# MoE expert weights of a two-layer encoder: gate and up matrix loaded as one array of 32 KB rows into four alternating places

## Chip, cores and metric

One core of one Trainium2 chip. The metric is the device time of one execution in microseconds (us). The profile is of one such execution.

## The reference, cut to what matters

All values are float32: x is 256 tokens by 1024. Each of the two layers is a token mixer (attention in layer 0, gated linear attention in layer 1) with a residual, then a hierarchical mixture of experts (MoE) with a residual:

```python
def hierarchical_moe(h, w_grp, b_grp, w_exp, b_exp, w_gate, w_up, w_down):
    ...   # top 1 of 4 groups, top 2 of its 8 experts: gates[token, expert]
    for e in range(N_EXPERTS):                       # 32 experts
        hid = jax.nn.silu(h @ w_gate[e]) * (h @ w_up[e])         # 1024 x 512 each
        y = y + gates[..., e:e + 1] * (hid @ w_down[e])          # 512 x 1024
```

Each of the three matrices of an expert is 2 MB (2^20 bytes to the MB where sizes of matrices are told), so a layer reads 32 x 6 = 192 MB of expert weights, which fit on the chip only a few at a time.

## The kernel before

**Rounds.** A layer's MoE runs in 11 rounds, r = 0 to 10. A light round handles three experts with 32 token slots each, round 8 (`HEAVY_ROUND`) the two experts with the most tokens, with 64 slots each. Experts 0 to 5 are taken in rounds 0 and 1 whatever the routing says; the list `order`, which DVE works out from the routing, names the later ones.

**TensorE in a round** (`expert_round`). `expand("gate")`: 24 products of 512 columns (48 matmul records), the weights as the moving operand. Then `scatter` of the round before into the sum (8 records, 96x512), `turn_gates` in even rounds, `expand("up")`, four transposes of `hid` (L2334), in odd rounds `gather` of the tokens of the next group (`ahead`), and the product with down (48 records). Round 0 is written apart (`expand_first`): gate and up in four quarters of the contraction.

**Places in SBUF.** `unit[0..8]` are nine places of 2 MB (16 KB on each of 128 partitions): gate in 0 to 2, up in 3 to 5, down in 6 to 8. The mixers use units 0 to 5 for their input projection and units 3 and 4 for the output projection. Two more places, `held` and `held_down`, lie in the arena that the mixers share; in each layer they take gate and down of expert 3 for round 1 and then stay empty until the next layer.

**What sets the order of the loads.** All of them are issued by SP in program order, on one queue. Each waits for a semaphore that TensorE raises when a kind of matrix has been used: `used["gate"]`, `used["up"]`, `used["down"]` (in round 0 also `quarter_used` and `up_quarter_used` after each quarter). SP blocks at the first wait that isn't met, and what stands behind it in the program isn't issued. In `later_round` SP waits for gate of the round before and issues three gates, waits for up and issues three ups, waits for down and issues three downs. On the other side TensorE waits for each kind's arrival alone (`arrived`). `second_round` refills the places of round 0 quarter by quarter for round 1, and then loads the first expert of round 2 in advance.

Of the kernel before, what the change touches and what calls it, by code (L numbers as in the profile page):

```python
# [19 lines left out]
P = 128  # L20
F32 = mybir.dt.float32
I32 = mybir.dt.int32
ALU = mybir.AluOpType
# [3 lines left out]
SEQ, D = 256, 1024  # L27
TILES = SEQ // P
KT = D // P
# [25 lines left out]
KINDS = ("gate", "up", "down")  # L55

# [5 lines left out]
GROUP = 2 * LIGHT  # L62
GROUP_SLOTS = 2 * ROUND_SLOTS
# [10 lines left out]
UNIT = 8 * HALF  # L74
IN_UNITS = 6
# [128 lines left out]
def by_block(w):  # L204

    layers = w.shape[0]
    return np.ascontiguousarray(w.reshape(layers, EXPERTS, KT, P, D_EXPERT).transpose(0, 1, 3, 2, 4)
                                ).reshape(layers, EXPERTS, P, UNIT)
# [10 lines left out]
def build(nc, A, out):  # L219
    ctx = ExitStack()  # L220
    with ctx:
# [145 lines left out]
        gfin = held[:, 0:D]  # L367
        y = hn
        moe_sum = hn
        up_rows_of = (up_rows, hn.rearrange("p t n -> p (t n)"))  # L370
# [4 lines left out]
        held_full = sem("held_full")  # L375
        held_down_full = sem("held_down_full")
        quarter_used, up_quarter_used, up_early_full = sem("quarter_used"), sem("up_quarter_used"), sem("up_early_full")
        up_rows_full = sem("up_rows_full")
        early_full = sem("early_full")
        first_full = [sem(f"first_full{b}") for b in range(2)]  # L380
        last_full = [sem(f"last_full{i}") for i in range(len(LAST_PARTS))]
        last_up = [sem(f"last_up{h}") for h in range(2)]
# [54 lines left out]
        class PassSems:  # L437


            def __init__(self, name, started, apart, held):  # L440
# [6 lines left out]
                self.held = held  # L447
                self.full = {kind: sem(f"{name}_{kind}_full") for kind in KINDS}
# [21 lines left out]
        main = PassSems("main", 0, {"gate": 2, "up": LIGHT, "down": 2 + LIGHT}, {"gate": 2, "up": 0, "down": 2})  # L470
        more = PassSems("more", 1, {"gate": 0, "up": 0, "down": 0}, {"gate": 0, "up": 0, "down": 0})
# [10 lines left out]
        OUT_UNITS = (3, 4)  # L482
# [64 lines left out]
        def _(sp):  # L547
# [3 lines left out]
            def mixer_weights(layer):  # L551

                for c in range(IN_UNITS):
                    if layer == 1:
                        sp.wait_ge(main.used[KINDS[c // 3]], ROUNDS)
# [17 lines left out]
                for c in range(LIGHT):  # L573
                    sp.wait_ge(proj_psum, 2 * IN_UNITS * layer + 2 * c + 2)
                    known(layer, "gate", c, unit[SLOT["gate"] + c], main.full["gate"])
                    if layer and c == 0:
                        half_rows(layer, "up", 0, 0, up_rows_of[0], up_rows_full)
# [1878 lines left out]
```

## Time and profile before

| | |
|---|---|
| three runs | 1180.72, 1181.81, 1183.72 us; median 1181.81 |
| the profiled execution | 1182.63 us, of it 1180.8 us between its first and last instruction |
| busy | TensorE matmul (PE) 84%, weight loads (PEld) 39%, DVE 24%, ACT 11%, POOL 1% |
| chain of work that ended last | PE 50%, DMA 43%, DVE 3%, SP 2% |
| HBM | 440.5 MB read, 374 GB/s over the span |

The span is cut in 40 slices of 29.5 us in the profile's second part: a digit is a busy share in tenths. Layer 0's MoE runs from about 156 to 583 us, layer 1's from 745 to 1172 us. In the timelines a row is a group of consecutive instructions of one engine: start, duration from the first start to the last end, engine and line, operation, operands and count, and in brackets the idle time before it and who ended it. "SPq ... DMA_DIRECT2D" is SP issuing a DMA. The view of busy time by stretch has, in each row: start and end, length, busy us and count of instructions of PE, PEld, DVE, ACT and POOL, the granted clock of TensorE as a share, the busy share of the 16 DMA engines, and GB/s.

### The profile page before, as it was taken

To read this page: it belongs to the slowest core of one execution; us is meant where nothing else is said; L and a number is where in the kernel's file an instruction comes from. 1 tells how busy PE (TensorE), PEld (TensorE's weight loads), DVE (VectorE), ACT (ScalarE), POOL (GpSimd) and SP (SyncE) were. 2 spreads that over 40 slices of the span, in tenths; PEclk is the share of its full clock that TensorE was granted. 3 is DMA by queue.
4 is the path that set the end of the run, shared out by engine and by line. 5 is a ranking of instruction groups with operands and counts; after the bars stand their busy time and mean duration, and the time that the engine had idled before them with its cause. 6 is when DMAs were issued, how large, how long until landed. Compare 5 with 4: busy or idle time off the path is not lost.

```text
span 1180.8 us, 12753 instructions
## 1 busy us (share of the span) xinstructions
PE 994.1 (84%) x5268; PEld 455.1 (39%) x5268; DVE 288.1 (24%) x677; ACT 125.9 (11%) x307; POOL 7.1 (1%) x12
## 2 busy tenths in 40 slices
PE   9999999966776777977999999999667767788876
PEld 8675653323223223342484546433132132232422
DVE  1265352201101101220322453522111111112212
ACT  2024010000000000000231121100000000000002
POOL 0000000000000000000000000000000000000000
PEclk9999999989879879988999999999898898899888
DMA  9923999999999999999983528899999999999995
GB/s 368 409 81 135 420 360 428 426 428 428 428 427 428 429 427 427 427 424 423 413 353 136 214 72 369 331 428 427 427 428 429 428 428 428 428 428 426 424 422 225
DMA packets 39297, 442.43 MB, mean 375 GB/s; under 512 B 4386, under 2 KB 4770, under 8 KB 11972
## 3 DMA queue, kind: packets, MB, share of 16 engines
q1 hardware_dynamic: 39092, 441.47, 89.7%
q8 instruction: 40, 0.66, 0.2%
q10 hardware_dynamic: 144, 0.12, 0.0%
q14 instruction: 21, 0.17, 0.0%
HBM read 440.53 MB, written 1.05 MB: 374 GB/s over the span
## 4 chain that ended last, share of the span: by engine, by line
PE 50%; DMA 43%; DVE 3%; SPq 2%; issue 2%; ACT 0%; DVEq 0%; POOL 0%
PE psum L1739 48%; DMA sb_weights<-moe_w_down 38%; DMA sb_weights<-moe_w_gate 5%; SPq L673 1%; SPq L679 1%; DMA sb_lead<-lead 0%; PE psum L2334 0%; DVE sb_weights L1598 0%; PE psum L1917 0%; PE psum L1750 0%; DVE sb_x L1618 0%; PE psum L1777 0%; PE psum L2112 0%; PE psum L2015 0%; PE psum L2202 0%
## 5 line engine op out<-in xcount | busy, mean ns | idle before, releaser
L1739 PE MATMUL psum<-sb_weights,sb_hT 128*32 128x512 f32 (+3 forms) x2352 | 468.7, 627 | 99.8 <-DMA sb_weights<-moe_w_gate 61.2
L1739 PE MATMUL psum<-sb_weights 128*32 128x512 f32 (+12 forms) x1632 | 318.7, 560 | 46.1 <-DMA sb_weights<-moe_w_down 41.0
L1739 PEld LDWEIGHTS psum<-sb_weights,sb_hT 128*32 128x32 f32 (+2 forms) x2352 | 148.1, 128 | 392.3 <-issue 313.5
L1739 PEld LDWEIGHTS psum<-sb_weights 128*32 128x32 f32 (+7 forms) x1632 | 115.8, 138 | 237.2 <-issue 195.3
L1611 DVE TENSOR_TENSOR sb_hn<-sb_hn,psum 128x512 f32<-128x512 f32 x72 | 49.5, 687 | 228.2 <-PE psum L1739 228.0
L1739 PE MATMUL psum<-sb_hT,sb_weights 128*128 128x256 f32 (+1 forms) x400 | 88.8, 380 | 0.1
L1739 PEld LDWEIGHTS psum<-sb_hT,sb_weights 128*128 128x128 f32 (+1 forms) x400 | 74.0, 187 | 12.6 <-issue 1.6
L1739 PE MATMUL psum<-sb_weights,sb_x 128*128 128x192 f32 (+2 forms) x448 | 69.6, 313 | 6.7 <-issue 6.1
L1739 PEld LDWEIGHTS psum<-sb_weights,sb_x 128*128 128x128 f32 x448 | 66.7, 197 | 11.5 <-issue 10.3
L1603 DVE COPY sb_weights<-psum 96x512 f32<-96x512 f32 (+1 forms) x20 | 13.7, 686 | 181.0 <-PE psum L1739 181.0
L1598 DVE TENSOR_TENSOR sb_weights<-sb_weights,psum 96x512 f32<-96x512 f32 (+1 forms) x22 | 15.0, 683 | 148.9 <-PE psum L1739 148.9
L920 ACT ACTIVATE sb_weights<-psum 96x512 f32<-96x512 f32 (+1 forms) x22 | 13.1, 594 | 353.9 <-PE psum L1739 353.9
L924 ACT ACTIVATE sb_weights<-psum 128x384 f32<-128x384 f32 (+1 forms) x22 | 11.0, 501 | 219.8 <-PE psum L2334 219.8
L1564 DVE TENSOR_TENSOR sb_hT<-psum,sb_lead 128x384 f32<-128x384 f32 (+1 forms) x40 | 21.2, 531 | 47.8 <-PE psum L1739 47.8
L2334 PE MATMUL psum<-sb_lead,sb_weights 96*128 96x96 f32 (+1 forms) x88 | 15.9, 303 | 19.0 <-DVE sb_weights L1598 19.0
L926 ACT ACTIVATE sb_weights<-psum 96x512 f32<-96x512 f32 (+1 forms) x22 | 13.1, 594 | 171.9 <-PE psum L1739 171.9
L2334 PEld LDWEIGHTS psum<-sb_lead,sb_weights 96*128 96x128 f32 (+1 forms) x88 | 12.3, 212 | 38.3 <-DVE sb_weights L1598 38.3
L1611 DVE TENSOR_TENSOR sb_x<-sb_x,psum 128x512 f32<-128x512 f32 x12 | 8.3, 688 | 51.7 <-PE psum L1739 51.7
L1739 PE MATMUL psum<-sb_lead 128*128 128x128 f32 (+3 forms) x28 | 8.8, 460 | 6.7 <-issue 6.7
L1195 DVE TENSOR_TENSOR sb_x<-sb_x,psum 128x512 f32<-128x512 f32 x6 | 4.1, 687 | 29.6 <-PE psum L1739 29.6
L801 ACT ACTIVATE sb_weights<-sb_weights 128x256 f32<-128x256 f32 x16 | 8.0, 500 | 26.5 <-DVE sb_weights L1104 26.5
L914 ACT ACTIVATE sb_weights<-psum 96x512 f32<-96x512 f32 (+1 forms) x12 | 6.7, 559 | 35.8 <-PE psum L2202 35.8
(210 smaller groups left out, 374.4 us busy)
## 6 DMA issues: line engine op xcount, KB each, us to landing
sb_weights<-moe_w_gate SPq DMA_DIRECT2D x60, 2048.0 KB, 24.5
sb_weights<-moe_w_down SPq DMA_DIRECT2D x58, 2048.0 KB, 27.1
sb_weights<-moe_w_up SPq DMA_DIRECT2D x48, 2048.0 KB, 27.1
sb_weights<-moe_w_up SPq DMA_DIRECT2D x22, 1024.0 KB, 22.1
sb_weights<-od_w_in_units SPq DMA_DIRECT2D x6, 2048.0 KB, 27.6
sb_weights<-ev_w_in_units SPq DMA_DIRECT2D x5, 2048.0 KB, 24.8
sb_weights<-moe_w_gate SPq DMA_DIRECT2D x16, 512.0 KB, 6.0
sb_weights<-moe_w_up SPq DMA_DIRECT2D x16, 512.0 KB, 8.0
```

The costliest lines, as they stand in the source:

```text
L673: sp.dma_start(unit[SLOT[kind] + k][:, at], src[:, at]).then_inc(last_full[i], 16)
L679: sp.dma_start(unit[SLOT[kind] + k], src).then_inc(s.full[kind], 16)
L801: nc.scalar.activation(pr[:, u % 2, m * SEQ:(m + 1) * SEQ], sc[:, u % 2, m * SEQ:(m + 1) * SEQ], ACT.Exp, bias=negmax[:, 2 * u + m:2 * u + ...
L920: nc.scalar.activation(hid[0:rows], psum[0:rows, 0], ACT.Silu).then_inc(s.silu_done, 1)
L924: nc.scalar.activation(hidT[:, 0:FT * rows], psum[:, 4, 0:FT * rows], ACT.Copy).then_inc(s.hidT_done, 1)
L926: nc.scalar.activation(ysel[0:rows, 0:HALF], psum[0:rows, 2], ACT.Copy).then_inc(s.y0_done, 1)
L1564: nc.vector.tensor_tensor(hsel[:, 2 * b:2 * b + 2, 0:slots], psum[:, GATHER_BANKS[b], 0:2 * slots].rearrange("p (j s) -> p j s", j=2), gai ...
L1598: nc.vector.tensor_tensor(hid[0:rows], hid[0:rows], psum[0:rows, 1], ALU.mult).then_inc(s.hid_done, 1)
L1603: nc.vector.tensor_copy(ysel[0:rows, HALF:D], psum[0:rows, 3]).then_inc(s.y1_done, 1)
L1611: nc.vector.tensor_tensor(xs, xs, psum[:, SCATTER_BANKS[i]], ALU.add).then_inc(s.x_added, 1)
L1739: return nc.tensor.matmul(o, l, r, start=start, stop=stop, skip_group_check=True)
L2334: ins = nc.tensor.transpose(psum[:, 4, f * rows:(f + 1) * rows], hid[0:rows].rearrange("p (c f) -> p f c", f=FT)[:, f, :], ident[0:rows, 0 ...
```

## The change

1. **One array for gate and up.** The host interleaves gate and up of an expert by blocks of the contraction into `moe_w_pair`: 32 KB on each partition, 4 MB in all. Block j holds gate's 512 columns, then up's.
2. **Four places of 4 MB.** `pair[0..2]` are units 0-1, 2-3 and 4-5, `pair[3]` is where `held` and `held_down` were. `pair_places(r)` gives a round its places: 0, 1, 2 in even light rounds, 3, 1, 2 in odd ones; 0, 1 in round 8; 2, 3, 0 in round 9; 1, 2, 3 in round 10. Down keeps its three units. The output projection now lies in units 4 and 5.
3. **Waits.** A pair is loaded when *up* of the last round that used its place is done; TensorE waits for all pairs of a round ahead of gate (`pairs_arrived`).
4. **Seven known experts.** Expert 6 can't be one of the two heavy ones any more (`KNOWN`), so it is loaded without the list. In `second_round` each quarter of round 0 that has been used releases quarters of experts 4, 6 and, from the third on, 5. Expert 2 comes in three parts (two quarters apart, `rows_place`, and a half) instead of the halves of experts 0 and 1.
5. **Last round.** Gate and up come in three pieces of rows (blocks 0-3, 4-5, 6-7) instead of a whole gate and up in two halves; TensorE scatters the round before first, then works through the pieces.
6. `gate_weights` (layer 1's small arrays, which lie in `pair[3]`) waits for the last up, and `gfin` moves out of `held`.

The diff, cut to its core:

```diff
@@ build @@
-        SLOT = {"gate": 0, "up": 3, "down": 6}
+        DOWN = IN_UNITS
         arena = weights[:, IN_UNITS * UNIT:]
-        held = arena[:, 3 * UNIT:4 * UNIT]
-        held_down = arena[:, 4 * UNIT:5 * UNIT]
+        pair = [weights[:, i * PAIR:(i + 1) * PAIR] for i in range(3)] + [arena[:, 3 * UNIT:5 * UNIT]]
 ...
+        def pair_places(r):
+
+            if r == HEAVY_ROUND:
+                return 0, 1
+            if r == HEAVY_ROUND + 1:
+                return 2, 3, 0
+            if r == LAST:
+                return 1, 2, 3
+            return 3 if r % 2 else 0, 1, 2
 ...
@@ second_round @@
+                for q in range(4):
+                    at = slice(q * PAIR_QUARTER, (q + 1) * PAIR_QUARTER)
+                    if q < 3:
+                        sp.wait_ge(quarter_used, 3 * layer + q + 1)
+                    else:
+                        sp.wait_ge(main.used["up"], layer * ROUNDS + 1)
+                    pair_quarter(layer, LIGHT + 1, q, pair[1][:, at], main.pair_full[1])
+                    if q >= 2:
+                        pair_quarter(layer, LIGHT + 2, q, pair[2][:, at], main.pair_full[2])
+                    pair_quarter(layer, GROUP, q, pair[0][:, at], main.pair_full[0])
+                sp.wait_ge(main.used["down"], layer * ROUNDS + 1)
+                for k in range(LIGHT):
+                    known(layer, "down", LIGHT + k, unit[DOWN + k], main.down_full)
 ...
@@ later_round @@
-                for kind in KINDS:
-                    sp.wait_ge(s.used[kind], n)
-                    w = A["moe_w_" + kind][layer]
 ...
+                w = A["moe_w_pair"][layer]
+                for i, (first, end) in enumerate(LAST_ROWS if columns else ((0, KT),)):
+                    at = slice(first * 2 * HALF, end * 2 * HALF)
+                    for k, (e, place) in enumerate(zip(es, pair_places(r))):
+                        if s is main and r == 2 and k == 0:
+                            continue
+                        if i == 0:
+                            sp.wait_ge(s.used["up"], n - r + round_before(r, place) + 1)
+                        src = w[bass.ds(e, 1)].rearrange("e p n -> p (e n)")
+                        sp.dma_start(pair[place][:, at], src[:, at]
+                                     ).then_inc(last_rows[i] if columns else s.pair_full[place], 16)
+                sp.wait_ge(s.used["down"], n)
 ...
@@ expert_round @@
+                def pairs_arrived():
+
+                    for place in here:
+                        loads = k * signals(s, place, LAST) + signals(s, place, r if g is None else 2 + h)
+                        if g is not None:
+                            loads = loads + (g - 1) * (2 if place in (1, 2) else 1)
+                        pe.wait_ge(s.pair_full[place], loads * 16)
+
+                def down_arrived():
 ...
+                elif columns:
                     scatter(s, n - 1, 1 - h, 0)
                     scatter(s, n - 1, 1 - h, 1)
+                    for i, (begin, end) in enumerate(LAST_ROWS):
+                        pe.wait_ge(last_rows[i], 16 * LIGHT * (k + 1))
+                        for bank, kind in enumerate(("gate", "up")):
+                            expand(kind, bank, range(begin, end))
+                else:
+                    pairs_arrived()
+                    expand("gate", 0)
+                    if prior:
+                        scatter(s, n - 1, 1 - h, 0)
+                        scatter(s, n - 1, 1 - h, 1)
                 if turn and not first:
```

How the loads stand on SP around rounds 1 and 2 of layer 0. Names in brackets are the semaphores that the row waits for; `TENSOR_LOAD sb_order` and the ISA rows read an expert's number from the list. Before (rounds 1's last loads, then round 2's):

```order
L649 DMA sb_weights<-moe_w_gate 128x4096
L596 DMA sb_weights<-moe_w_down 128x4096 [waits main_down_used]
L596 DMA sb_weights<-moe_w_down 128x4096
L649 DMA sb_weights<-moe_w_down 128x4096
L605 TENSOR_LOAD sb_order [waits routed]
...
L679 ISA [waits main_gate_used]
L679 DMA sb_weights<-moe_w_gate 128x4096
L679 ISA
L679 DMA sb_weights<-moe_w_gate 128x4096
L679 ISA [waits main_up_used]
L679 DMA sb_weights<-moe_w_up 128x4096 x3
L679 DMA sb_weights<-moe_w_down 128x4096 [waits main_down_used]
```

In the change (from the last quarters of round 1 to the downs of round 2):

```order
L625 DMA sb_weights<-moe_w_pair 128x2048 [waits main_up_used]
L625 DMA sb_weights<-moe_w_pair 128x2048 x2
L620 DMA sb_weights<-moe_w_down 128x4096 [waits main_down_used]
L620 DMA sb_weights<-moe_w_down 128x4096 x2
L629 TENSOR_LOAD sb_order [waits routed,ordered]
...
L679 ISA [waits main_up_used]
L679 DMA sb_weights<-moe_w_pair 128x8192
L679 ISA [waits main_up_used]
L679 DMA sb_weights<-moe_w_pair 128x8192
L687 ISA [waits main_down_used]
L687 DMA sb_weights<-moe_w_down 128x4096
```

Round 2's two gates were released by gate of round 1 and its ups by up; now both pairs (8192 columns of 4 bytes) wait for up, and the first expert's whole pair has moved ahead of `order`, into the quarters.

TensorE in round 2: the start of gate, then `turn_gates` (96x128), up, and the transposes of `hid`. Before:

```order
L2282 ISA [waits main_gate_full]
L1739 MATMUL psum<-sb_weights,sb_hT 32x512 [waits main_hsel_done]
L1739 MATMUL psum<-sb_weights,sb_hT 32x512 x5
...
L2202 MATMUL psum<-sb_lead,sb_weights 96x128 [waits main_sel_done]
L2202 MATMUL psum<-sb_lead,sb_weights 96x128 x3
L2265 ISA
L1739 MATMUL psum<-sb_weights,sb_hT 32x512 [waits main_up_full]
L1739 MATMUL psum<-sb_weights,sb_hT 32x512 x23
L2332 REGISTER_ALU
L2334 MATMUL psum<-sb_lead,sb_weights 128x96 [waits main_hid_done]
L2334 MATMUL psum<-sb_lead,sb_weights 128x96 x3
```

In the change:

```order
L2270 ISA [waits main_pair0_full]
L2270 ISA [waits main_pair1_full]
L2284 ISA [waits main_pair2_full]
L1746 MATMUL psum<-sb_weights,sb_hT 32x512 [waits main_hsel_done]
L1746 MATMUL psum<-sb_weights,sb_hT 32x512 x5
...
L2209 MATMUL psum<-sb_lead,sb_weights 96x128 [waits main_sel_done]
L2209 MATMUL psum<-sb_lead,sb_weights 96x128 x3
L1746 MATMUL psum<-sb_weights,sb_hT 32x512 x24
L2345 REGISTER_ALU
L2347 MATMUL psum<-sb_lead,sb_weights 128x96 [waits main_hid_done]
L2347 MATMUL psum<-sb_lead,sb_weights 128x96 x3
```

The wait for up's arrival ahead of up is gone; all three places of the round are waited for ahead of gate, where one wait for the gates stood.

## Rows read from the trace of the kernel before

**Rows 1.** Page, second part: granted TensorE clock and DMA rate in 40 slices

```profile
PEclk9999999989879879988999999999898898899888
GB/s 368 409 81 135 420 360 428 426 428 428 428 427 428 429 427 427 427 424 423 413 353 136 214 72 369 331 428 427 427 428 429 428 428 428 428 428 426 424 422 225
```

**Rows 2.** Page, fourth part: shares of the chain that ended last

```profile
PE 50%; DMA 43%; DVE 3%; SPq 2%; issue 2%; ACT 0%; DVEq 0%; POOL 0%
```

**Rows 3.** Busy time by stretch: rows of 8, 4, 16 KB

```profile
142.00:154.00 12.00, 11.85 (x83) 10.56 (x83) 7.70 (x40) 3.12 (x8) 0.00 (x0) 1.00 1.00 417
174.00:182.00 8.00, 8.00 (x66) 4.54 (x67) 4.12 (x13) 0.81 (x2) 0.00 (x0) 1.00 1.03 415
261.00:305.00 44.00, 32.60 (x188) 13.14 (x185) 6.82 (x11) 1.68 (x3) 0.00 (x0) 0.92 1.01 428
```

**Rows 4.** The same view, round 0 of layer 0 and of layer 1

```profile
156.00:174.00 18.00, 17.20 (x115) 5.78 (x109) 8.97 (x41) 0.86 (x2) 1.80 (x1) 1.00 0.92 322
747.00:769.00 22.00, 21.20 (x151) 9.31 (x148) 12.87 (x52) 1.08 (x2) 1.80 (x1) 1.00 0.95 344
```

**Rows 5.** Timeline of SP, layer 0, rounds 0 to 2

```profile
159.59 0.33 SPq L639 DMA_DIRECT2D sb_weights<-moe_w_up  x1
163.77 0.33 SPq L639 DMA_DIRECT2D sb_weights<-moe_w_up  x1
171.38 1.38 SPq L639 DMA_DIRECT2D sb_weights<-moe_w_up  x3
184.32 0.81 SPq L596 DMA_DIRECT2D sb_weights<-moe_w_down  x2
185.23 0.38 SPq L649 DMA_DIRECT2D sb_weights<-moe_w_down  x1
192.79 0.89 SPq L679 DMA_DIRECT2D sb_weights<-moe_w_gate  x2
204.13 1.28 SPq L679 DMA_DIRECT2D sb_weights<-moe_w_up  x3
```

**Rows 6.** Line 649 at 185.23 us: time from issue to landing

```profile
DMA to landing us min/median/max: 18.6/18.6/18.6
```

**Rows 7.** Stretches after an empty queue: one 2 MB DMA issued at 111.10 us

```profile
111.00:113.00 2.00, 1.48 (x25) 1.08 (x24) 1.86 (x4) 1.98 (x7) 0.61 (x1) 1.00 0.73 123
113.00:115.00 2.00, 1.91 (x34) 1.54 (x32) 1.60 (x13) 1.43 (x5) 0.00 (x0) 1.00 0.79 319
115.00:117.00 2.00, 2.00 (x14) 1.03 (x9) 1.97 (x9) 0.00 (x0) 0.00 (x0) 1.00 0.98 418
```

**Rows 8.** Page, sixth part: two loads that began on an empty queue

```profile
sb_weights<-od_w_out_units SPq DMA_DIRECT2D x2, 2048.0 KB, 8.1
```

**Rows 9.** Timeline of PE: rounds 1 to 3 and 7, layer 0

```profile
196.47 7.07 PE L1739 MATMUL psum<-sb_weights,sb_hT 128*32 128x512 f32 x48
204.96 5.39 PE L1739 MATMUL psum<-sb_weights,sb_x 128*128 128x192 f32 x32
210.29 7.07 PE L1739 MATMUL psum<-sb_weights 128*32 128x512 f32 x48
224.15 3.89 PE L1739 MATMUL psum<-sb_weights 96*128 96x512 f32 x8
227.88 0.60 PE L2202 MATMUL psum<-sb_lead,sb_weights 128*96 128x128 f32 x4
236.34 0.72 PE L2334 MATMUL psum<-sb_lead,sb_weights 96*128 96x96 f32 x4 [0.87 <-DVE sb_weights L1598]
252.97 8.82 PE L1739 MATMUL psum<-sb_weights,sb_hT 128*32 128x512 f32 x48 [7.54 <-DMA sb_weights<-moe_w_gate]
452.52 3.76 PE L1739 MATMUL psum<-sb_weights,sb_x 128*128 128x128 f32 x32
```

**Rows 10.** Busy time by stretch around the start of round 3's gate, layer 0

```profile
249.00:257.00 8.00, 4.03 (x18) 1.06 (x21) 0.00 (x0) 0.00 (x0) 0.00 (x0) 0.57 1.01 428
```

**Rows 11.** Timeline of PE: the slowest gate, layer 1, round 7

```profile
1018.86 9.87 PE L1739 MATMUL psum<-sb_weights,sb_hT 128*32 128x512 f32 x48 [5.98 <-issue]
```

More of the change, by code:

```diff
@@ L62 @@
 GROUP = 2 * LIGHT
+KNOWN = GROUP + 1
 GROUP_SLOTS = 2 * ROUND_SLOTS
@@ L74 @@
 UNIT = 8 * HALF
+PAIR = 2 * UNIT
+PAIR_QUARTER = PAIR // 4
 IN_UNITS = 6
@@ L468, in __init__, with signals @@
                 self.x_added = sem(name + "_x_added")
-        main = PassSems("main", 0, {"gate": 2, "up": LIGHT, "down": 2 + LIGHT}, {"gate": 2, "up": 0, "down": 2})
-        more = PassSems("more", 1, {"gate": 0, "up": 0, "down": 0}, {"gate": 0, "up": 0, "down": 0})
+        main = PassSems("main", 0, LIGHT)
+        more = PassSems("more", 1, 0)
+        def signals(s, place, r):
+            pieces = {(0, 2): 4, (1, 1): 4, (2, 0): 0, (2, 1): 3, (1, LAST): 0, (2, LAST): 0, (3, LAST): 0} if s is main else {}
+            return sum(pieces.get((place, q), 1) for q in range(r + 1) if place in pair_places(q))
         past_if = sem("past_if")
@@ L583, in mixer_weights @@
                         sp.wait_ge(qe_done, 2 * C_HEADS)
-                        known(layer, "down", 0, unit[SLOT["down"]], main.full["down"])
+                        known(layer, "down", 0, unit[DOWN], main.down_full)
             def gate_weights():
+                sp.wait_ge(main.used["up"], ROUNDS)
                 sp.dma_start(wgf.rearrange("p j c -> p (j c)"), A["od_low_rank"]).then_inc(gates_loaded, 16)
@@ L625, in second_round @@
             def second_round(layer):
-                for part in range(4):
-                    rows = slice(part * 2 * HALF, (part + 1) * 2 * HALF)
-                    for kind, used, early, first in (("gate", quarter_used, held_full, 1),
-                                                     ("up", up_quarter_used, up_early_full, 2 if part < 2 else 0)):
-                        if part < 3:
-                            sp.wait_ge(used, 3 * layer + part + 1)
-                        else:
-                            sp.wait_ge(main.used[kind], layer * ROUNDS + 1)
-                        for k in range(first, LIGHT):
-                            src = A["moe_w_" + kind][layer, LIGHT + k]
-                            sp.dma_start(unit[SLOT[kind] + k][:, rows], src[:, rows]
-                                         ).then_inc(main.full[kind] if part == 3 else early, 16)
@@ L2343, in expert_round @@
                 if not columns:
-                    arrived("down")
-                us = [unit[SLOT["down"] + e] for e in range(experts)]
-                if holds:
-                    pe.wait_ge(held_down_full, 16 * (k + 1))
-                    us[0] = held_down
+                    down_arrived()
+                us = [unit[DOWN + e] for e in range(experts)]
                 if columns:
```

180 lines of the change are left out of this document (70 added, 110 removed).

## Prediction

> **What bounds the kernel now.** I read the slices first. In both MoE stages, slices 7 to 19 and 27 to 39, the DMA moves 423 to 429 GB/s without a break, while between them, in the mixers, it is partly or wholly idle [rows 1]. The chain gives PE 50% and DMA 43% of the span [rows 2]; the DMA share is the expert rounds, the PE share the mixers and the first two rounds. So a layer's MoE ends when its last byte has arrived, plus a fixed tail, and that moment is: the last time at which the DMA queue was empty, plus the bytes still to come divided by the rate. A change to the loads can act in three ways only: on the rate, on holes in the queue after the mixer, and on TensorE's path where that becomes longer than the transfers. A light round loads 18 MB, 18.87 million bytes, 44.1 us at 428 GB/s [rows 3]; TensorE is busy for about 33 of 44 us in such a stretch [rows 3].
>
> What counts as noise: about 0.3%, 3.5 us, for a comparison of these two kernels.
>
> **The rate.** The same view gives 428 GB/s with 16 KB rows, 417 with 8 KB and 415 with 4 KB [rows 3]. If each row costs a fixed time beside its bytes, the step from 4 to 16 KB puts 32 KB at 430 and the step from 8 to 16 KB at 434. Per layer 22 of the 32 pairs go as whole 32 KB rows inside the busy stage (all but experts 0 to 6 and the last round's three), 92.3 million bytes, 215.6 us at 428. At 430 that saves 1.0 us, at 434 3.0 us; below, 0, if the chip cuts such rows. I take 1.6 a layer, nearer the 4 KB end because that stretch holds nothing but 4 KB rows. The rule of the Trainium skill (DMA: Bandwidth & Descriptors, Where 436 GB/s comes from) sets the ceiling at 435 GB/s; an estimate with it is at most 3.5 us a layer. No row here shows that ceiling. The quarters of round 0 are 8 KB now where they were 4 KB, but TensorE sets their pace.
>
> **The hole that is closed and the one that opens.** In round 0 the queue isn't full: 322 GB/s over 18 us in layer 0, 344 over 22 us in layer 1 [rows 4], a loss of 4.5 and 4.3 us against 428. The change releases up to 3 MB a quarter there instead of 2.5, and expert 6 needs no list. Both versions put 10 MB on the queue between round 0's first quarter and its end, and then three downs, 6 MB, when down of round 0 has been used, at 184.3 us [rows 5]. What differs is what comes next.
>
> Before, gates of round 2 are issued at 192.8, when gate of round 1 is done, ahead of the third down's landing at 185.23 + 18.6 = 203.8 [rows 5, 6]. The queue never empties, and the third down's bytes are in at about 202.7 (a DMA that starts on an empty queue lands 8.1 us after its issue [rows 8]: some 2.0 us until it moves at full rate, below, 4.9 us of bytes at 428, and 1.1 us until TensorE may use it).
>
> In the change gate no longer releases anything, and both pairs of round 2 wait for up of round 1. Up ends at 196.47 + 7.07 = 203.5 [rows 9], with nothing on the engine ahead of it waiting for a DMA, and SP issues at 204.1 [rows 5]. When is the queue empty? The first quarters are issued at 159.6, when up's first quarter is done [rows 5], at an empty queue; effective start 161.6. 10 MB in 8 KB rows at 417 to 428 take 24.5 to 25.1 us, so 186.4; the later quarters come 4.2 us apart (159.59, 163.77, the last at 171.4 [rows 5]) and are in time. Then 14.7 us of downs: 201.1. Nothing more is on the queue until 204.1. **The restart** costs more than the gap: after the lone issue at 111.10 the next 6 us carried 123, 319 and 418 GB/s over 2 us each [rows 7], 1.72 million bytes, 4.0 us at 428; the transfer as good as began at 113.0, 1.9 us after its issue. With 2.0, the DMA goes on at 206.1 where before it was at the same byte at 202.7. **Term 1: +3.4 us a layer**, the closed hole included. Here the Trainium skill speaks more gently (DMA: Bandwidth & Descriptors, Anatomy of one DMA and Latency): a fixed cost of about 2 us per DMA, most of it after the last byte, and about 0.6 us to the first byte of a DMA that SP issues. The rows put most of it ahead of the bytes. By the page's 0.6 as an estimate, term 1 would be about 2 and terms 2 to 4 almost nothing, which comes out a little under rival (a) below.
>
> **Term 2: light rounds 3 to 7 and the first half of round 8.** Call T the moment at which a round's pairs have landed; their last bytes came in at T - 1.1. Behind them stand that round's downs, 14.7 us, and the first pair of the next round, 9.7, issued right behind the downs since its place is free: the queue lasts until T + 23.3. The next 8 MB come when up is done. By T TensorE will have been idle for some 9 us (round period 43.8, less 20.4 to up, 1.6 to the end of the transposes, 5.4 of `gather` and 7.1 of down) in odd rounds and 13 to 14 in even ones, without the gather (before, 7.5 [rows 9]). After 7.5 us the granted clock was 0.57 over the 8 us around the restart, mostly the half level, 1.2 of 2.4 GHz [rows 10], and gate took 8.82 us instead of 7.07 [rows 9], 9.87 at the worst [rows 11]. I take 9.5. Then scatter 3.9, `turn_gates` 0.6 in even rounds, up 7.1 [rows 9]: T + 21.0 or T + 20.4. That is 2.3 to 2.9 us before the queue is empty, against the 2.0 of a restart: nearly hidden, but the 16 DMA engines don't run dry at one moment. Bounds: 0, and 1 us each. I take 0.3, six times: **+2 us**, and the same in layer 1.
>
> **Term 3: the heavy round's downs.** They wait for down of round 7. From T: up done at T + 20.4, 0.9 until the transposes, 0.7 of them, `gather` ahead 3.8, down 7.1 [rows 9]: T + 32.9. Behind round 7's downs and the first pair of round 8 only one pair more follows: the queue ends at T + 33.1. So the restart shows nearly whole: **+2 us** (0 to 3). Before, round 8's ups would still be on the queue. What is queued behind on SP are the first two pairs of round 9, which start later by the same.
>
> **Term 4: the last round.** Its places 2 and 3 wait for up of round 9, place 1 is free early, so only 2 MB (4.9 us) and round 9's downs (14.7) cover: until T + 18.5. Round 9 has no scatter; up ends at T + 9.5 + 0.6 + 7.1 = T + 17.2 [rows 9]. **+1 us** (0 to 2). The three pieces themselves cost nothing: 3.5 us of products and about 4 us to `hidT` follow the last piece, while down's first half takes 7.3 us more to come. Without that cover each microsecond would go to the end.
>
> **Edits at nothing.** Output weights in units 4 and 5: the second is issued when unit 5 is free and lands as up of expert 2 did there, 8 us later, about a microsecond ahead of its use; with that cover gone it would delay the mixer by as much as it is late. The wait in `gate_weights`: SP stands there while 6 MB of downs (14.7 us) are still on the queue. The other register and semaphore instructions run on engines that wait for DMA. The heavy round stays the same work.
>
> **The sum.** 3.4 + 2 + 2 + 1 - 1.6 = 6.8 us a layer, 13.6 for two, since layer 1's mixer starts when layer 0 ends. Against the profiled execution's 1182.6 that is 1196.2; the median is 0.8 lower, so **1195.5 us**. With each term at its bounds: 2 x (3.4 - 3.0) = +1 to 2 x (3.4 + 6 + 3 + 2) = +29.
>
> **Rivals.** (a) *Restarts stay hidden*: only term 1 and the rate count. 2 x (3.4 - 1.6) = +3.6, 1185.4, on the border of what can be told. For it: slacks of 2.3 to 2.9 us against 2.0. Against it: round 8, where no slack is left. (b) *TensorE becomes the bound of every round.* If the half clock lasts longer after the longer idle time, the path from T to up passes T + 23 and each round pays in full. Decides at a gate of some 11 us; 1.5 us more in six rounds and 2 layers is +18 on top, 1213. For it: idle times up to 14 us, which no row of these rounds shows. Against: the worst gate is 9.87 [rows 11]. (c) *Faster*: the hole of round 0 is closed and none opens. The price is 4.5 less the 2.0 of the one restart that stays, plus 1.6 of the rate, 4 us a layer: 1174. It decides where up of round 1 ends before about 199 instead of 203.5. Against it stands that this stretch of TensorE is unbroken work of gate, scatter and up [rows 9]. For it, rates nearer 434 would carry part of the way alone. (d) *Rows of 32 KB are moved no faster than 16 KB ones*: +3.2 on the forecast, 1199, inside its range.
>
> **How the numbers follow.** Forecast with (d), 1188 to 1204: 0.60. Rival (a), 1182 to 1188: 0.15. Rival (b), 1204 to 1225: 0.14. Rival (c), 1170 to 1181: 0.11. The range 1181 to 1212 leaves out (c) and half of (b), 0.18. Faster by over 0.3% (under 1178.3): most of (c), 0.10. Within 0.3%: the rest of (c) and half of (a), 0.12. Slower: 0.78.
>
> **What would show it.** In the stretch view of layer 0 a hole at about 201 to 206 us and none at 156 to 174 except its first 3 us; pairs of round 2 issued at about 204; TensorE idle ahead of every gate and never ahead of up; a rate of 430 or more in rounds 3 to 6; a dip in the rate some 34 us after round 7's gate begins. The forecast is wrong if up of round 1 ends before 200, if the rate over rounds 2 to 7 stays below 425 (b), or if there is no dip at round 8 (a).

## The result, and the profile after

| | before | changed kernel |
|---|---|---|
| median, range | 1181.95 us, 1180.72 to 1183.72 (4 runs) | 1213.9 us, 1210.34 to 1214.35 (4 runs) |
| ratio | | 1.0256, 95% interval 1.0238 to 1.0274 |
| span of the profiled execution | 1180.8 us | 1212.0 us |

The change costs 32 us; the forecast was 13.6. The direction was right, the forecast size less than half of what came, and 1213.9 lies above the stated range of 1181 to 1212.

The page of the changed kernel, second part (DMA rate in 40 slices of 30.3 us) and fourth (shares of the chain); before: [rows 1, 2].

```profile
GB/s 367 321 165 144 428 291 376 416 431 426 426 434 423 429 422 426 403 423 353 417 249 174 267 81 388 344 361 431 424 419 433 422 431 429 423 395 431 389 325 265
PE 64%; DMA 30%; issue 2%; DVE 1%; SPq 1%; ACT 0%; DVEq 0%
```

In the slices of the expert rounds, where 422 to 429 stood without a break, there are now dips: 376, 403 and 353 in layer 0, 361, 395, 389 and 325 in layer 1. The slice with round 0, which had a dip before (360 and 331), went to 291 in layer 0 and to 344 in layer 1. TensorE's share of the chain went from 50% to 64%. The view of busy time by stretch puts a size on the holes; a hole is a stretch in which the DMA engines move less than the 428 GB/s of a full queue:

```profile
153.00:170.00 17.00, 16.44 (x115) 9.96 (x113) 7.32 (x35) 3.58 (x6) 0.00 (x0) 1.00 0.51 188
206.00:215.00 9.00, 8.13 (x55) 4.85 (x50) 1.71 (x3) 0.49 (x1) 0.00 (x0) 1.00 0.64 244
486.00:493.00 7.00, 4.64 (x19) 1.43 (x14) 0.69 (x1) 0.00 (x0) 0.00 (x0) 0.76 0.84 312
546.00:556.00 10.00, 8.53 (x55) 2.60 (x52) 0.68 (x1) 0.49 (x1) 0.00 (x0) 0.92 0.56 216
806.00:815.00 9.00, 8.13 (x57) 4.46 (x52) 1.24 (x2) 0.49 (x1) 0.00 (x0) 1.00 0.52 193
1087.00:1093.00 6.00, 2.07 (x10) 0.58 (x6) 0.69 (x1) 0.00 (x0) 0.00 (x0) 0.77 0.83 300
1147.00:1161.00 14.00, 12.52 (x89) 3.84 (x83) 0.68 (x1) 1.64 (x3) 0.00 (x0) 1.00 0.37 137
```

A row's loss is its length times (1 - GB/s / 428): 9.5 us around the start of round 0 of layer 0, which comes 6.6 us late; 3.9 and 4.9 us after round 1 of the two layers; 1.9 and 1.8 us at the heavy rounds; 5.0 and 9.5 us at the last rounds. The last pair is the largest, and the prediction had it at 1 us each.

The other surprise comes before any expert round, in layer 0's mixer. SP issues the output weights' second half at 111.63, and TensorE waits for it. The timelines of SP and of PE:

```profile
87.33 24.63 SPq L603 DMA_DIRECT2D sb_weights<-ev_w_out_units  x2
111.63 0.33 SPq L603 DMA_DIRECT2D sb_weights<-ev_w_out_units  x1
```

```profile
119.27 6.17 PE L1746 MATMUL psum<-sb_weights,sb_hT 128*128 128x512 f32 x8 [3.43 <-DMA sb_weights<-ev_w_out_units]
```

The timeline of PE in the kernel before, at the same place:

```profile
113.88 1.42 PE L1739 MATMUL psum<-sb_weights 128*64 128x96 f32 x24
115.23 3.70 PE L1739 MATMUL psum<-sb_weights,sb_hT 128*128 128x512 f32 x8
118.77 1.04 PE L1956 MATMUL psum<-sb_lead,sb_hn 128*128 128x128 f32 x8
120.22 10.14 PE L1739 MATMUL psum<-sb_weights,sb_hT 128*128 128x512 f32 x23 [0.41 <-DVE sb_hT L1184]
```

The output projection begins at 115.23 there, not at 120: what starts at 120.22 is its second group. It starts 4.0 us later now (0.5 of them stand already ahead of the wait), and its first 8 records take 6.17 us instead of 3.70. Round 0 of layer 0 starts at 162.43 where it was 155.83, 6.6 us late; layer 1's mixer loses nothing more (17.7 us late at its start, 17.8 at its end). The changed kernel's second profile, of the run again below, shows the same wait and the same slow records: 3.57 us idle, then 6.71 us.

### The profile page after: what moved, and what is told of

Same layout as the page of the kernel before. It is cut to its first block, busy times and chain, and to the rows that moved or that the text cites. A ratio compares the mean times of both kernels' runs of the same rounds, so it can differ in the third digit from the quotient of the medians.

```text
span 1212.0 us, 12709 instructions
## 1 busy us (share of the span) xinstructions
PE 985.4 (81%) x5268; PEld 453.5 (37%) x5268; DVE 288.1 (24%) x677; ACT 125.9 (10%) x307; POOL 7.1 (1%) x12
## 4 chain that ended last, share of the span: by engine, by line
PE 64%; DMA 30%; issue 2%; DVE 1%; SPq 1%; ACT 0%; DVEq 0%
PE psum L1746 63%; DMA sb_weights<-moe_w_pair 25%; DMA sb_weights<-moe_w_down 4%; DMA sb_weights<-ev_w_out_units 1%; DMA sb_weights<-ev_w_in_units 1%; SPq L687 1%; SPq L679 0%; PE psum L2347 0%; PE psum L2209 0%; DVE sb_weights L1605 0%; DVE sb_x L1625 0%; PE psum L1924 0%; PE psum L1784 0%; ACT sb_weights L933 0%; PE psum L2119 0%
## 5 line engine op out<-in xcount | busy, mean ns | idle before, releaser
L1746 PEld LDWEIGHTS psum<-sb_weights,sb_hT 128*32 128x32 f32 (+2 forms) x2352 | 151.1, 129 | 463.8 <-issue 379.6
L1746 PE MATMUL psum<-sb_weights 128*32 128x512 f32 (+12 forms) x1632 | 307.3, 537 | 12.6 <-ACT sb_weights L933 6.4
L1746 PEld LDWEIGHTS psum<-sb_weights 128*32 128x32 f32 (+7 forms) x1632 | 110.8, 135 | 196.9 <-issue 164.9
L1746 PEld LDWEIGHTS psum<-sb_hT,sb_weights 128*128 128x128 f32 (+1 forms) x400 | 74.0, 187 | 13.6 <-issue 1.6
```

Of the source, the lines that this page charges most:

```text
L1746: return nc.tensor.matmul(o, l, r, start=start, stop=stop, skip_group_check=True)
```

## The experiments

**What the late output weights cost.** TensorE waits for the first array at the projection's start, for the second at the third group, the first that reads it.

```diff
-                pe.wait_ge(out_full, 32 * (layer + 1))
+                pe.wait_ge(out_full[0], 16 * (layer + 1))
...
                     if i == 2:
+                        pe.wait_ge(out_full[1], 16 * (layer + 1))
                         turn_x(layer, 1, 0)
```

> Only TensorE's wait for layer 0's output weights is eased: the first array alone is waited for at the start of the output projection, the second at its third product group. In the changed kernel the projection waited 3.43 us for the second array and its first 8 records took 6.17 us instead of 3.70. Theory A (the step 'output weights at nothing' failed, and all that follows is shifted by it): projection starts at about 115.8, its first 8 records take about 3.7 us, round 0 of layer 0 starts at about 156 instead of 162.43, time 1213.9 - 6.0 = 1208, by 5.5 to 6.6 us. Rival B: the delay is absorbed, since round 0's last quarters wait for their own 2 MB (issued at the end of the projection) and the DMA sets the pace from there: 1212 to 1214.

1206.7 us, ratio 1.0199 (1.0183 to 1.0215): 7.2 us less, a little over theory A's 5.5 to 6.6; the two profiled executions are 5.7 apart. Its timeline of PE:

```profile
115.57 3.70 PE L1746 MATMUL psum<-sb_weights,sb_hT 128*128 128x512 f32 x8
```

Start and length are what theory A gave; round 0 begins at 156.3. Next to nothing was absorbed: round 0 starts 6.2 us earlier, and layer 1's mixer 5.5 us earlier (596.81 instead of 602.28).

A second experiment keeps the wait and fills it: four products of 384 columns on an unused bank ahead of it, in layer 0.

```diff
+                if layer == 0:
+                    keep_warm(*[384] * 4, bank=4)
                 pe.wait_ge(out_full, 32 * (layer + 1))
```

> Four products of 384 columns on an unused bank are put into TensorE's wait ahead of layer 0's output projection; nothing is loaded or released otherwise. Theory A (of what the late output weights cost, some 2.5 us are the 8 records that ran at the half clock after the wait, 6.17 us against 3.70): the projection still starts at 119.2 to 119.3, its first 8 records take 3.7 us, time 1213.9 - 2.5 = 1211.4. Rival B: the records are slow for another reason or the shift is absorbed: 1213 to 1215.

The timeline of PE shows the four products (8 records) and the projection's start. Behind it are the stretches of busy time with these records, of the changed kernel and of this one; the granted clock is 0.50 in the first (1.2 of 2.4 GHz) and 1.00 in the second:

```profile
116.72 2.85 PE L1746 MATMUL psum<-sb_lead 128*128 128x384 f32 x8
120.24 3.70 PE L1746 MATMUL psum<-sb_weights,sb_hT 128*128 128x512 f32 x8 [0.68 <-DMA sb_weights<-ev_w_out_units]
```

```profile
121.00:123.00 2.00, 2.00 (x4) 0.83 (x3) 0.00 (x0) 0.00 (x0) 0.00 (x0) 0.50 1.00 426
```

```profile
121.00:123.00 2.00, 2.00 (x6) 0.84 (x5) 0.00 (x0) 0.00 (x0) 0.00 (x0) 1.00 0.97 377
```

The records take 3.70 us again: after 3.43 us of idle time TensorE ran them at the lower of its clock levels, and without the idle time it didn't. This profile runs 1.0 us late already ahead of the products (SP issues the second half at 112.58 instead of 111.63), so the projection starts at 120.24, not at 119.27. The time, 1211.7 us (1209.5 to 1217.3), ratio 1.0260 (1.0240 to 1.0279), can't be told from the changed kernel's. So the split of the 6.6 us, about 4 of start and 2.5 of clock, rests on the rows alone.

**The last round.** Round 9 alone takes blocks 0 to 3 of gate and of up, then blocks 4 to 7; the first pieces of the last round are released after the first half.

```diff
+                elif halves:
+                    pairs_arrived()
+                    expand("gate", 0, range(0, 4))
+                    expand("up", 1, range(0, 4)).then_inc(half_used, 1)
...
+                        if columns and before == r - 1:
+                            if i == 0:
+                                sp.wait_ge(half_used, layer + 1)
+                            elif i == 1 and k == 1:
+                                sp.wait_ge(s.used["up"], n)
```

> Round 9 alone takes blocks 0 to 3 of gate and up, then blocks 4 to 7, and the first pieces of the last round are released after the first half instead of after all of up. Theory A (the empty queue at 547 to 555 us, 5.0 us lost, and at 1148 to 1160 us, 9.5 us lost, is what TensorE's path round 8 down, gather, gate, up costs): release about 7 us earlier, both holes go but for about 1 us each, the rest of each MoE comes earlier by as much: 1213.9 - 12.5 = 1201, by 11 to 14 us. Rival B: behind the hole TensorE's own path through the last pieces is what ends the MoE, so that a fuller queue brings only 0 to 4 us: 1210 to 1214.

1204.9 us, ratio 1.0185 (1.0169 to 1.0200): 9.0 us less, between theory A's 11 to 14 and rival B's 0 to 4, and nearer to A. Both holes are closed (first and last row), in the same view:

```profile
546.00:556.00 10.00, 8.52 (x56) 2.68 (x53) 0.68 (x1) 1.64 (x3) 0.00 (x0) 0.95 1.00 428
803.00:813.00 10.00, 9.13 (x62) 5.35 (x57) 1.80 (x3) 0.49 (x1) 0.00 (x0) 1.00 0.61 231
1085.00:1092.00 7.00, 5.32 (x34) 1.73 (x29) 0.69 (x1) 0.00 (x0) 0.00 (x0) 1.00 0.74 269
1141.00:1161.00 20.00, 18.53 (x124) 5.62 (x119) 1.22 (x2) 2.23 (x4) 0.00 (x0) 1.00 1.00 424
```

14.5 us of holes went and 9.0 us came: 2.9 in layer 0 (layer 1's mixer starts at 599.36 instead of 602.28), where the hole was 5.0, and 6.0 in layer 1, where it was 9.5. The third row shows a part of the difference: the hole at the heavy round of layer 1 is 2.6 us instead of 1.8. The second shows none: the hole after round 1 is 4.6 us, much as before. The rest stays open.

**The hole after round 1 (term 1).** Round 1 alone in halves, with `half_used` raised ahead of its scatter; the two pairs of round 2 come in halves.

```diff
+                if s is main and r == 2:
+                    for half in range(2):
+                        at = slice(half * UNIT, (half + 1) * UNIT)
+                        if half:
+                            sp.wait_ge(s.used["up"], n)
+                        else:
+                            sp.wait_ge(half_used, layer + 1)
+                        for e, place in zip(es[1:], (1, 2)):
+                            src = w[bass.ds(e, 1)].rearrange("e p n -> p (e n)")
+                            sp.dma_start(pair[place][:, at], src[:, at]).then_inc(s.pair_full[place], 16)
```

> Round 1 alone takes blocks 0 to 3 of gate and up, then the scatter and blocks 4 to 7; the pairs of round 2 come in halves of 16 KB rows, the first released after the first half. Theory A (term 1 of the prediction stands: the empty queue after round 1, 207 to 214 us and 807 to 814 us, costs 4.5 and 5.1 us): both holes go, 1213.9 - 9.6 = 1204.3, by 8 to 10 us. Rival B (TensorE, idle for longer and at half clock, has become the bound of rounds 3 to 8): what is gained at round 2 is lost again as longer waits of the queue before round 9: 1211 to 1214.

1206.35 us, ratio 1.0196 (1.0180 to 1.0211): 7.6 us less, 3.8 a layer, just under theory A's 8 to 10. The stretches that held the two holes:

```profile
202.00:215.00 13.00, 12.13 (x77) 6.18 (x77) 3.18 (x5) 1.08 (x2) 0.00 (x0) 1.00 1.01 434
802.00:815.00 13.00, 12.13 (x84) 7.33 (x81) 3.23 (x6) 1.08 (x2) 0.00 (x0) 1.00 1.01 430
```

**The rate of 32 KB rows.** Every whole pair as two DMAs of 16 KB rows, issued at the same moment.

```diff
-                        sp.dma_start(pair[place][:, at], src[:, at]
-                                     ).then_inc(last_rows[i] if columns else s.pair_full[place], 16)
+                        for at in [at] if columns else [slice(x * UNIT, (x + 1) * UNIT) for x in range(2)]:
+                            sp.dma_start(pair[place][:, at], src[:, at]
+                                         ).then_inc(last_rows[i] if columns else s.pair_full[place], 16)
```

> Every whole pair of rounds 2 to 9 is issued as two DMAs of 16 KB rows one after the other, at the same moment as before; nothing else. Theory A (rows of 32 KB are worth 1.6 us a layer, as the prediction had it; the packets of 32 KB took 1213 ns in the middle, those of 16 KB 612): 1213.9 + 3 = 1217, by 2 to 4 us slower. Rival B (32 KB rows are moved no faster than 16 KB ones): 1213 to 1215. Rival C (pieces keep the 16 engines more even, and the queue's restart is softer): faster by 1 to 3 us.

1211.6 us, ratio 1.0244 (1.0230 to 1.0258). The changed kernel was timed again on the same chip as two later variants:

> The changed kernel once more, unaltered, as the measure for its variants on the same chip: 1212 to 1215, ratio to the kernel before 1.0256 within 0.0015 by both theories. If it came out at 1211.6, the variant with two DMAs of 16 KB rows (1.0244) would be the same as it; if at 1214 or more, 32 KB rows have cost something.

It came to 1215.2 us (1210.0 to 1215.6), ratio 1.0256 (1.0237 to 1.0274), as the first time. The intervals of the ratios overlap, so two DMAs are the same or a little faster (1.4 us by the ratios, 2.3 and 3.6 by the medians); theory A, 2 to 4 us slower, falls. Three stretches show how, first with 32 KB rows, then with 16 KB:

```profile
235.00:298.00 63.00, 46.07 (x261) 13.09 (x255) 8.51 (x13) 2.87 (x5) 0.00 (x0) 0.88 1.01 432
349.00:393.00 44.00, 28.57 (x164) 11.54 (x161) 6.17 (x10) 1.08 (x2) 0.00 (x0) 0.84 0.99 423
905.00:1075.00 170.00, 114.42 (x657) 36.98 (x654) 21.13 (x34) 7.41 (x13) 0.00 (x0) 0.86 1.00 428
```

```profile
235.00:298.00 63.00, 46.30 (x264) 13.45 (x258) 8.03 (x13) 2.87 (x5) 0.00 (x0) 0.87 1.01 428
349.00:393.00 44.00, 28.62 (x164) 11.97 (x161) 5.79 (x9) 1.08 (x2) 0.00 (x0) 0.84 1.01 428
905.00:1075.00 170.00, 115.29 (x660) 37.26 (x661) 21.31 (x34) 7.41 (x13) 0.00 (x0) 0.86 1.00 427
```

32 KB rows reach 432 GB/s where the queue stays full (431 at 815 to 898 us, against 428), inside the 430 to 434 that the prediction allowed. The packets say the same: one of 32 KB takes 1213 ns and one of 16 KB 612, so 16 engines would move 432 and 428 GB/s (an estimate from these durations). But in the second row a dip at a restart (360 to 393 GB/s from 387 to 391 us) takes it back, and over the longest stretch 428 against 427 is left.

**Do the losses add?** Output weights in units 3 and 4 as before the change (the second half of expert 1 and the first half of expert 5 come in after them), and rounds 1 and 9 in halves.

> The three repairs together: output weights in the third and fourth of the six 2 MB units (expert 1's second half and expert 5's first half then come into them, expert 2's second half early), round 1 in halves, round 9 in halves. Theory A (the three losses are separate pieces of one chain, so their gains add: 7.2, 9.0 and 7.5 us): 1213.9 - 23.7 = 1190. Rival B (they share a bound, TensorE's longer path in rounds 3 to 8, and the queue runs empty elsewhere instead): 1194 to 1200.

1191.7 us, ratio 1.0075 (1.0062 to 1.0088): 22.2 us less against 23.8 for the three alone. Taken from the ratios, which compare each kernel with the one before on its own chip, they are 6.7, 8.4 and 7.1 us alone and 21.4 together, each to within about 3 us. They are nearly independent.

**Every round in halves**, on top of that, with two DMAs of 16 KB rows for each pair (term 2).

> As the three repairs together, and besides every round from 1 to 9 takes blocks 0 to 3 of gate and up first, then 4 to 7; each pair comes as two DMAs of 16 KB rows, the first released when the first half is used. Theory A (what is left are the small gaps at up's end in every second round and ahead of the heavy round, 0.5 to 1.5 us each, some 7 us in two layers, which an earlier release covers): 5 us under the kernel with the three repairs, about 1185. Rival B (those gaps have no part in the time, since the 16 DMA engines catch up): equal to it, 1189 to 1191. Rival C (16 KB rows cost what the 32 KB rows gave): 1 to 3 us slower than it.

1187.5 us, ratio 1.0040 (1.0027 to 1.0053), 4.2 us less, near theory A's 5. Two things were changed at once here, the halves and the 16 KB rows. The remaining holes:

```profile
157.00:164.00 7.00, 6.90 (x50) 2.61 (x52) 1.07 (x3) 0.00 (x0) 0.00 (x0) 1.00 0.34 111
475.00:484.00 9.00, 7.12 (x46) 2.23 (x42) 0.69 (x1) 0.59 (x1) 0.00 (x0) 1.00 0.69 253
1068.00:1075.00 7.00, 4.76 (x24) 1.33 (x20) 0.69 (x1) 0.00 (x0) 0.00 (x0) 0.84 0.73 267
```

**The heavy round's downs (term 3).** 3.7 and 2.6 us are lost in the last two rows. Half of round 9's first pair, whose place is free since round 7, is issued ahead of these downs.

```diff
+                if s is main and r == HEAVY_ROUND:
+                    early_half(layer, main.pair_full[2], expert_at(HEAVY_ROUND * LIGHT))
                 sp.wait_ge(s.used["down"], n)
```

> As the kernel with every round in halves (1187.5), and besides the first 2 MB of round 9 (half of its first pair, whose place is free since up of round 7) are issued ahead of the heavy round's downs instead of behind them. Theory A (term 3 of the prediction: the heavy round's downs find an empty queue, 3.6 us lost at 476 to 483 us in layer 0 and 2.5 us at 1069 to 1074 us in layer 1): both gaps go, 1187.5 - 5.5 = 1182, by 4 to 6 us. Rival B (the heavy round's downs, 4.9 us later, then hold up TensorE and with it all that round 8 releases): 1186 to 1190.

1182.9 us (11 runs), ratio 1.0004 (0.9995 to 1.0014), 4.6 us less, inside theory A's 4 to 6: as fast as the kernel before. The two stretches:

```profile
465.00:495.00 30.00, 27.52 (x150) 11.75 (x152) 6.14 (x11) 1.96 (x4) 0.00 (x0) 1.00 1.01 426
1060.00:1090.00 30.00, 26.39 (x129) 8.82 (x130) 4.88 (x8) 2.06 (x4) 0.00 (x0) 1.00 1.01 426
```

**Round 0's hole.** Round 0 takes block 0 of gate and up before block 1, and the first loads are released after it.

```diff
+                        for steps in ((0,), (1,)) if frees and q == 0 else ((2 * q, 2 * q + 1),):
```

> As the kernel with the heavy round's cover, and besides round 0 takes block 0 of gate and up before block 1, and the first loads of round 0 are released after block 0 (0.5 MB each of two experts) instead of after both blocks. Theory A (a layer's loads stand until TensorE has used the first quarter of gate and up together, 3.7 us of products where the kernel before released gates after 1.9): the empty queue at 157 to 164 and 749 to 756 us shrinks by some 1.8 us a layer, 3 us under the other kernel. Rival B (the third and fourth quarter release what counts, and an earlier start is only waited away): equal to it within 1 us.

1183.8 us (12 runs), ratio 1.0012 (1.0001 to 1.0023): no gain, rival B. Busy time by stretch, the kernel without this edit first:

```profile
157.00:163.00 6.00, 6.00 (x43) 2.04 (x40) 0.36 (x1) 0.00 (x0) 0.00 (x0) 1.00 0.43 146
```

```profile
157.00:167.00 10.00, 10.00 (x71) 3.44 (x68) 2.18 (x8) 0.00 (x0) 1.80 (x1) 1.00 0.80 287
184.00:193.00 9.00, 8.32 (x61) 2.27 (x52) 1.71 (x3) 0.59 (x1) 0.00 (x0) 1.00 0.94 348
```

4.0 us at the start of round 0 became 3.3, and 1.7 are lost at 184 to 193, ahead of round 1's downs, where it was 0.7 without the edit (397 GB/s). Those downs wait for down of round 0 and go out at 184.96 instead of 184.69, so TensorE's path through round 0 sets where the stream starts for good.

**The final gain's products in layer 1.** Why was the last hole 9.5 us in layer 1 and 5.0 in layer 0? `spread_gain` stands on that path in layer 1 alone.

```diff
-                if layer:
-                    spread_gain()
...
+                if held_gate and k:
+                    spread_gain()
+                    pe.wait_ge(gfin_done, 2)
                 expert_round(s, k, HEAVY_ROUND, k * MOE_GROUPS + EARLY_GROUPS, 0, heavy=True, turn=True)
```

> The changed kernel with one thing moved: in layer 1 TensorE's 16 small products that spread the final gain (3.8 us, between the branch after round 8 and the gather for round 9) run ahead of round 8 instead, where TensorE waits 3.9 us for the heavy pairs. Theory A (the last round's empty queue ends when TensorE has done round 9's up, so what stands on that path counts in full: 9.5 us in layer 1 against 5.0 in layer 0, where these products are absent): the gap at 1148 to 1160 us shrinks to 5.5 us, 1213.9 - 4 = 1210. Rival B (the gap is set by something else, or round 8 now starts later by as much): 1213 to 1215.

1212.6 us (1210.8 to 1214.5), ratio 1.0251 (1.0235 to 1.0266): not told from the changed kernel. The hole did shrink to 4.6 us, but not by the 3.8 us of products that theory A counted. The timeline of PE in layer 1, in the changed kernel and then in this one:

```profile
1091.77 9.70 PE L1746 MATMUL psum<-sb_weights,sb_hT 128*64 128x512 f32 x32 [3.93 <-issue]
1132.05 3.79 PE L1746 MATMUL psum<-sb_lead 128*128 128x128 f32 x16 [6.20 <-issue]
1135.62 6.55 PE L1746 MATMUL psum<-sb_weights,sb_x 128*128 128x192 f32 x32
```

```profile
1089.95 7.09 PE L1746 MATMUL psum<-sb_weights,sb_hT 128*64 128x512 f32 x32 [0.82 <-ACT sb_weights L949]
1130.58 7.21 PE L1746 MATMUL psum<-sb_weights,sb_x 128*128 128x192 f32 x32 [9.15 <-DVE sb_weights L1536]
```

From the end of round 8's down to the end of the gather the path is 16.3 us in both: 6.20 + 3.6 + 6.5, and 9.15 + 7.2. The products ran beside a wait that was there anyway. What was won is at the heavy gate, which takes 7.09 us instead of 9.70: the products fill the wait ahead of it, and the granted clock from 1092 to 1094 us is 1.00 instead of 0.50. It also starts 1.8 us earlier, with the landing of its last pair (1089.7 instead of 1091.7); that wasn't the aim of the move, and its cause stays open.

What sets the size of the last hole is the way from the end of round 7's down, where the queue has just run empty in both layers, to the end of round 9's up, which releases the next loads. The same bytes are issued on that way in both layers. Layer 0's heavy gate in the changed kernel, to compare with layer 1's above:

```profile
479.85 7.07 PE L1746 MATMUL psum<-sb_weights 128*32 128x512 f32 x48
489.28 8.78 PE L1746 MATMUL psum<-sb_weights,sb_hT 128*64 128x512 f32 x32 [2.36 <-issue]
```

| profile, layer | way, us | last hole, us |
|---|---|---|
| changed kernel again, 0 | 63.9 | 4.0 |
| changed kernel, 0 | 64.6 | 5.0 |
| gain products moved, 1 | 65.2 | 4.6 |
| changed kernel, 1 | 68.9 | 9.5 |
| changed kernel again, 1 | 69.0 | 9.6 |

The 4.3 us between the layers are 1.6 of longer wait for the heavy pairs (3.93 against 2.36), 0.9 of slower gate (9.70 against 8.78) and 1.8 between down of round 8 and the end of the gather. That answers for the 4.5 us between the holes.

In the kernel with all repairs the same move changes nothing:

> All repairs in one kernel: the one with the heavy round's cover (1182.9, equal to the kernel before) and the final gain spread ahead of round 8. Theory A (with the queue full at the last round nothing on TensorE's path there counts any more): 1182 to 1184, the same as without the move. Rival B (TensorE's path still ends the last round in layer 1): 1179 to 1180, under both kernels.

1183.9 us (12 runs), ratio 1.0007 (0.9997 to 1.0016): theory A. No kernel of this study beats the one before.

## Why the forecast was too small, point by point

| step | forecast, both layers | measured |
|---|---|---|
| rate of 32 KB rows | -3.2 | 0 or a small loss (1.4 to 3.6 us less without them, not clear of noise) |
| term 1, hole after round 1 | +6.8 | 7.6 |
| term 2, light rounds | +4 | 4.2, 16 KB rows included |
| term 3, heavy round's downs | +4 | 4.6 |
| term 4, last round | +2 | 9.0 |
| output weights | 0 | 7.2 |

Terms 1, 3 and 4 and the output weights add to 28.4; with 4.2 for term 2 it is 32.6, against 32.0 measured. Taken away one on top of the other they come to 31.0, and then the kernel stands at the time of before. That the first sum meets the 32.0 so closely is partly luck, since each piece is good to about 3 us. Terms 2 and 3 were measured in kernels that already held the other repairs, and the halves may bring more than the change had cost.

**Two steps failed. The first: "Edits at nothing. Output weights in units 4 and 5", put at 0 and worth 7.2 us.** It said that the second array "lands as up of expert 2 did there, 8 us later, about a microsecond ahead of its use". It landed at 119.2, as reckoned. A microsecond behind that stands the row at 120.22, which only continues the projection, while the projection waits for both arrays ahead of its first product, at 115.23 in the kernel before. The text named the cover and the price if it were gone, and then read the wrong row. To the wait came TensorE's clock.

**The second and largest: term 4, "up ends at T + 17.2", put at 1 us a layer (0 to 2) and worth 9.0 us in both.** The step counts from the landing of round 9's pairs, with TensorE idle until then. It wasn't: here TensorE came last. In layer 0 round 9's gate starts with no wait at all, behind a 6.77 us stand after round 8 and the gather. The stand could be read before the change too, and no term held it. Timelines of PE in the kernel before, of PE in the changed kernel, and of SP there:

```profile
507.57 7.90 PE L1739 MATMUL psum<-sb_weights,sb_x 128*128 128x192 f32 x32 [6.08 <-issue]
```

```profile
529.22 7.74 PE L1746 MATMUL psum<-sb_weights,sb_x 128*128 128x192 f32 x32 [6.77 <-issue]
536.89 7.07 PE L1746 MATMUL psum<-sb_weights,sb_hT 128*32 128x512 f32 x48
544.46 7.07 PE L1746 MATMUL psum<-sb_weights,sb_hT 128*32 128x512 f32 x48
```

```profile
551.72 1.36 SPq L679 DMA_DIRECT2D sb_weights<-moe_w_pair  x3
1156.95 1.38 SPq L679 DMA_DIRECT2D sb_weights<-moe_w_pair  x3
```

Up ends at 551.5, and the three loads behind it go out at 551.72 with the queue nearly run out (49 GB/s in the microsecond from 550). In layer 1 the same chain, from the end of round 8's down to the end of up, is 30.9 us instead of 29.1, and the heavy gate ahead of it is later and slower, as shown above. Round 9, the round after the branch, had to be walked along TensorE and not along the loads.

**The rate.** The number was right for a full queue (431 and 432, against 430 to 434 allowed), the step from rate to time was not. My reading, which no run separates: in a kernel whose loads now wait for TensorE once a round, a faster transfer partly lengthens the gap.

**Term 1** was right in mechanism and place: pairs of round 2 were issued at 210.5, 204.1 plus the 6.4 us that round 1's up is late. Here the row-based 2.0 us for a restart held. By the 0.6 us of the Trainium skill (DMA: Bandwidth & Descriptors, Latency and other measured facts) the term would have been about 2 a layer, an estimate; 3.8 were measured. The about 2 us per DMA that the prediction took from the Trainium skill (same page, Anatomy of one DMA) are its fit for DMAs issued from GpSimd; these are issued by SP. "The closed hole included" was wrong: round 0's hole did not close. Its first loads wait for the first quarter of gate and up together, so they go out 3.7 us after round 0 starts instead of 2.0. In the kernel with the heavy round's cover the stretch from 156 to 174 us carries 322 GB/s, a loss of 4.5 us, exactly as before [rows 4]:

```profile
156.00:174.00 18.00, 17.11 (x113) 5.86 (x113) 8.89 (x41) 0.59 (x1) 1.80 (x1) 1.00 0.80 322
```

As the finer release showed, closing a part of it brings nothing, since the stream starts for good only behind down of round 0.

**Terms 2 and 3** held to within a microsecond (term 2 only if the 16 KB rows brought nothing, which isn't shown). TensorE was idle 8.3 to 15.3 us ahead of the gates of rounds 2 to 7, they took 8.7 to 9.3 us (9.5 was taken), and the dip at round 8 came some 33 us after round 7's pairs had landed.

**The rivals.** (a), (c) and (d) are out; for (d), rows of 32 KB are moved faster, but the time shows nothing of it. (b) gave 1213, the time that came, but that is luck, for its mechanism isn't there: the worst light gate took 9.3 us and the rounds kept their 44 us.

## What to carry to other kernels

When a load moves to a place that comes free later, look for the first instruction that waits for it, and read its start from the row in which that operation *begins*: a timeline splits one projection into several rows. A release by a larger unit (both matrices of an expert instead of one) has to be walked once for every round of another shape; here the regular rounds lost little, the irregular ones most. Working through a joint unit in halves, with a release after the first, gave back most of what joining had cost.

## What the runs showed of the hardware that I had not expected

**A stand at a branch.** In the stand after round 8, in layer 1, DVE shows 6.08 us between its last addition and the one-hot that the gather needs, with nothing it waits for in the profile; the extra-pass branch stands there. Timeline of DVE, changed kernel, layer 1:

```profile
1125.89 0.69 DVE L1618 TENSOR_TENSOR sb_hn<-sb_hn,psum 128x512 f32<-128x512 f32 x1 [0.17 <-PE psum L1746]
1132.65 0.56 DVE L1541 TENSOR_TENSOR sb_weights<-sb_lead,sb_weights 128x384 f32<-128x384 f32 x1 [6.08 <-issue]
```

It is in the kernel before too: DVE 6.48 us in layer 1, TensorE 6.08 and 6.67 us in layers 0 and 1. TensorE's stand is between 5.7 and 6.9 us wherever nothing else ends it. DVE's was 7.22 us in the kernel whose gain products were moved, but also 7.19 in the one with round 1 in halves, so that isn't from the move. In layer 0 DVE shows 0.83 us and TensorE alone stands. What the stand is made of wasn't tried.

**The lower clock.** It came in the work behind idle times of 3.4 and 3.9 us: 6.17 us instead of 3.70 for 8 records, 9.70 instead of 7.09 for a heavy gate; with products put into them, both ran at full clock. The length of the idle time alone doesn't sort the cases. Behind 2.36 us, ahead of layer 0's heavy gate, the granted clock was 0.50 from 490 to 492 us and the gate took 8.78 us; behind 3.34 us in the last round of layer 0 it stayed at 1.00, and 24 records took the 3.63 us of full speed:

```profile
580.14 3.63 PE L1746 MATMUL psum<-sb_weights,sb_hT 128*32 128x512 f32 x24 [3.34 <-DMA sb_weights<-moe_w_pair]
```
